# Packing the picks of 32 experts into 27 units of four 32-row strips, in a hybrid attention and mixture-of-experts layer

## What is computed

```python
def hier_moe(h, lw):
    t = h.reshape(B * S, D)
    g_prob, g_idx = lax.top_k(softmax(t @ w_router_group + b_group), 1)
    e_prob, e_idx = lax.top_k(softmax(logit_e_of_that_group), 2)
    weight = g_prob * e_prob / sum(e_prob)
    expert_id = g_idx * 8 + e_idx
    ...
def expert_block(xblk, e):                       # 128 rows, one expert
    hid = silu(xblk @ w_gate[e]) * (xblk @ w_up[e])    # 1024 -> 256
    return hid @ w_down[e]                             # 256 -> 1024
...
y[row_token] += yb * row_weight                  # each token gets two such rows
x = x + gt_m * y
```

## Time and profile before

| | |
|---|---|
| runs | 1118.38 us median of 3 (1114.22 to 3773.64) |
| profiled execution | 1115.39 us, of which the span of the trace is 1113.6 us |
| PE | busy 1042.7 us, 94% of the span |
| DVE, POOL, ACT | busy 57%, 27%, 24% of the span |
| DMA | 229.8 MB, mean 206 GB/s |

### The profile page before, as it was taken

The page is one execution under the profiler, slowest core; times in us unless marked ns, Lnnn a source line. Parts: engine busy times, 40 slices in busy tenths (PEclk is TensorE's granted clock), DMA queues, the critical chain, the costliest instruction groups (busy, mean ns, idle before and its releaser), DMA issues.

```text
span 1113.6 us, 14260 instructions
## 1 busy us (share of the span) xinstructions
PE 1042.7 (94%) x4861; PEld 692.3 (62%) x4861; DVE 632.0 (57%) x1261; ACT 268.0 (24%) x593; POOL 304.1 (27%) x350
## 2 busy tenths in 40 slices
PE   3789999999978899999999999999999999999994
PEld 0334555555556556667776675877777777777772
DVE  1455555555566655675766778456755444445443
ACT  1232222222251232323323212221111111111110
POOL 1122222222231110110110000234445455444444
PEclk9799999999998899999999999799999999999998
DMA  9793333333254322332321129668989999988950
GB/s 306 283 404 125 145 144 145 145 145 126 80 168 130 88 109 97 142 115 67 142 84 59 77 97 389 235 228 345 345 300 351 343 361 345 348 339 341 355 188 18
DMA packets 78102, 229.80 MB, mean 206 GB/s; under 512 B 29835, under 2 KB 33566, under 8 KB 62294
## 3 DMA queue, kind: packets, MB, share of 16 engines
q1 hardware_dynamic: 50608, 198.86, 47.7%
q0 software_dynamic: 24048, 26.81, 7.2%
q10 hardware_dynamic: 3382, 3.32, 0.9%
HBM read 201.23 MB, written 88.25 MB: 260 GB/s over the span
## 4 chain that ended last, share of the span: by engine, by line
PE 81%; DVE 9%; DMA 2%; POOL 2%; issue 2%; ACT 1%; ACTq 1%; DVEq 0%; SPq 0%; POOLq 0%
PE bank L1045 13%; PE bank L1405 10%; PE bank L1407 10%; PE bank L1422 10%; PE bank L998 9%; PE bank L1215 9%; PE bank L1159 6%; PE bank L1185 5%; PE bank L1126 2%; PE bank L1010 2%; PE bank L1026 2%; DMA grope<-in_g_knorm 1%; POOL st L845 1%; PE bank L1056 1%; PE bank L1237 1%
## 5 line engine op out<-in xcount | busy, mean ns | idle before, releaser
L1045 PE MATMUL bank<-W_in,hT 128*128 128x512 f32 (+3 forms) x480 | 172.7, 542 | 3.7 <-DMA W_in<-in_w_in 3.7
L844 POOL TENSOR_SCALAR st<-st 128x1 f32<-128x1 f32 (+5 forms) x76 | 17.6, 231 | 549.6 <-DVEq L1779 251.4
L1045 PEld LDWEIGHTS bank<-W_in,hT 128*128 128x128 f32 (+1 forms) x480 | 80.1, 185 | 91.6 <-issue 84.4
L1422 PE MATMUL bank<-WD,hidT 128*128 128x512 f32 x264 | 118.9, 593 | 1.7 <-DVE hidT L2436 1.7
L1405 PE MATMUL bank<-WG,xT 128*128 128x256 f32 x528 | 119.5, 379 | 1.0 <-DVE xT L2420 1.0
L1407 PE MATMUL bank<-WU,xT 128*128 128x256 f32 x528 | 119.3, 379 | 0.0
L1215 PE MATMUL bank<-W_out,mT 128*128 128x512 f32 (+1 forms) x288 | 115.4, 563 | 0.1
L1407 PEld LDWEIGHTS bank<-WU,xT 128*128 128x128 f32 x528 | 100.3, 190 | 13.6
L1405 PEld LDWEIGHTS bank<-WG,xT 128*128 128x128 f32 x528 | 97.7, 190 | 13.1 <-issue 1.2
L2200 DVE COPY probT<-bank 128x512 f32<-128x512 f32 (+3 forms) x100 | 56.3, 563 | 57.3 <-PE bank L998 50.1
L1185 PEld LDWEIGHTS bank<-vall,probT 128*128 128x128 f32 x616 | 76.8, 192 | 15.6 <-issue 14.6
(11 more groups left out here) (333 smaller groups left out, 1438.0 us busy)
## 6 DMA issues: line engine op xcount, KB each, us to landing
WG<-in_w_gate_e SPq DMA_DIRECT2D x33, 1024.0 KB, 7.0
WU<-in_w_up_e SPq DMA_DIRECT2D x33, 1024.0 KB, 9.4
WD<-in_w_down_e SPq DMA_DIRECT2D x33, 1024.0 KB, 12.9
ada_w<-in_w_ada SPq DMA_DIRECT2D x24, 1024.0 KB, 7.9
residual_scratch<-x_att SPq DMA_DIRECT2D x32, 512.0 KB, 4.4
kbuf<-k_scratch SPq DMA_DIRECT2D x12, 384.0 KB, 5.1
xbuf<-in_x_prompt SPq DMA_DIRECT2D x8, 512.0 KB, 3.8
W_in<-in_w_in SPq DMA_DIRECT2D x2, 2048.0 KB, 22.3
```

Of the source, the lines that this page charges most:

```text
L1045: ins = mm(out, hT[:, place_of[t] % 2, k, :R], W_in[:, k, c0 + c.start:c0 + c.stop], start=(k == 0), stop=(k == KD - 1))
L1422: ins = mm(psum[5 + half][:], hidT[:, k, :], WD[u][:, k, half * 512:(half + 1) * 512], start=(k == 0), stop=(k == 1))
```

## The change

Experts are ranked in each group by their picks in the six early tiles. The expert of rank r in its group gets `CAPS[r]` rows, 160, 128, 128, 128, 96, 96, 64 or 64, that is 27 x 128 rows for all four groups, in place of 32 x 128. The rows of one rank are laid one behind the other over the four groups and cut into units of four strips of 32 rows; the ranks come in the order 1, 6, 0, 2, 4, 7, 3, 5. So 27 units result: 14 of one expert, 7 of two halves (64 rows each), 6 of which one strip belongs to another expert than the other three. Picks beyond an expert's rows go to overflow blocks, up to 24, which all run in the loop; the static 33rd block is gone. What goes with it:

- `gu` and `down` issue one matmul for each run of strips: 128, 64 or 32 columns of the stationary rows, each with its own expert's weights, into the partitions of the bank that belong to these rows. Gate and up weights stand side by side (`WGU`) and are one matmul of 512 columns.
- Units 4, 5, 18 and 19 each bring two new experts, units 15 and 24 too; unit 10 none, the others one. SP reads the expert numbers (`order_i`) in the order `LOADS`, and refills the gate/up half of a slot when the last `gu` of its expert has ended, the down half when the last `down` has.
- DVE picks the early tiles' experts in heads 1 to 3 of the last attention step, PE counts them in head 5 (`rankA`), DVE sorts (`sort_experts`), looks up starts and limits (`expert_rows`) and places the early picks in heads 5 to 7. `place` and `code` get further small instructions.
- There is one copy of the residual rows. POOL gathers a unit's residual rows only when the scatter of each of the three units before it that shares a group with it (under another expert) has landed. The plan never puts such two units side by side; units 5, 6, 18, 19 and 20 have one at distance 2.
- POOL writes 64 more small constants at the start. The MoE part is no longer a loop but written out for all units.

The plan, and the rules for POOL:

```diff
+CAPS = (160, 128, 128, 128, 96, 96, 64, 64)
+RANKS = (1, 6, 0, 2, 4, 7, 3, 5)
+def strip_plan():
+    units, first = [], {}
+    for r in RANKS:
+        strips = [g for g in range(NG) for _ in range(CAPS[r] // STRIP)]
+        first[r] = len(units)
+        units += [[(r, g) for g in strips[i:i + SIDE]] for i in range(0, len(strips), SIDE)]
+    return units, first
+def clashing(m, n):
+    return any(g == h and r != s for r, g in UNITS[m] for s, h in UNITS[n])
...
+        def residual_rows(m):
+            if m >= NG:
+                scattered(m - NG)
+                g.wait_ge(s_ysc[m % NG], 32 * (m // NG))
+            for b in range(max(0, m - NG + 1), m):
+                if clashing(b, m):
+                    scattered(b)
+            rows_in(m % NG, at(TOKEN, m))
+        def gathered_before(m):
+            return max([m - 2] + [b + 1 for b in range(max(0, m - NG + 1), m) if clashing(b, m)])
```

SP and PE:

```diff
-        for z in z_d:
-            sp.dma_start(z[P * t:P * t + R], x_att[:R, s % 2]).then_inc(s_st2[f"x2_{s % 2}"], 16)
+        sp.dma_start(z_d[P * t:P * t + R], x_att[:R, s % 2]).then_inc(s_st2[f"x2_{s % 2}"], 16)
...
+        for q in range(3, len(LOADS)):
+            e = expert(q)
+            if q >= SLOTS:
+                sp.wait_ge(s_gu, LAST_USE[LOADS[q - SLOTS]] + 1)
+            load_gate_up(e, q % SLOTS)
+            if q >= SLOTS:
+                sp.wait_ge(s_down, LAST_USE[LOADS[q - SLOTS]] + 1)
+            load_down(e, q % SLOTS)
...
             for k in range(KD):
-                mm(psum[2][:, 0:DE], xT[:, k, :], WG[u][:, k, :], start=(k == 0), stop=(k == KD - 1))
-            for k in range(KD):
-                ins = mm(psum[3][:, 0:DE], xT[:, k, :], WU[u][:, k, :], start=(k == 0), stop=(k == KD - 1))
+                for c, n, x in runs(UNITS[m]):
+                    ins = mm(out[c:c + n], xT[:, k, c:c + n], WGU[LOADS.index(x) % SLOTS][:, :, k, :], start=(k == 0), stop=(k == KD - 1))
```

DVE, what `place` and `code` get (`place` the first two lines, `code` the rest):

```diff
+            do(TT(over, rankb[:, 0:n], bcast(limit[:].unsqueeze(1), [P, n, NE]), ALU.is_ge))
+            do(STT(rankb[:, 0:n], over, OVER, rankb[:, 0:n], ALU.mult, ALU.add))
...
+            do(V.tensor_copy(ovq_i[:, :, a:b], rank[:, :, a:b]))
+            rows_and_units(ovq_i[:, :, a:b], a, b)
+            do(TT(unit_hot[:, :, a:b], bcast(iota_f[:, 0:NU].unsqueeze(1).unsqueeze(1), [P, 2, n, NU]), bcast(at_f[:, 1, :, a:b].unsqueeze(3), [P, 2, n, NU]), ALU.is_equal))
```

More of the change, by code:

```diff
@@ L113, in free, with runs @@
         return self.freed[self.at[tag][0]]
+def clashing(m, n):
+    return any(g == h and r != s for r, g in UNITS[m] for s, h in UNITS[n])
+assert not any(clashing(m, m) or m and clashing(m, m - 1) for m in range(NU))
+def runs(unit):
+    starts = [i for i in range(SIDE) if i == 0 or unit[i] != unit[i - 1]]
+    width = SIDE if len(starts) == 1 else SIDE // 2 if starts == [0, SIDE // 2] else 1
+    return [(i * STRIP, width * STRIP, unit[i]) for i in range(0, SIDE, width)]
 def overflow_blocks(eng, n_ov, block):
-    with eng.If(n_ov > 1):
-        with eng.Fori(0, MAXOV - 1) as i:
-            with eng.If(i + 1 < n_ov):
-                block(i + 1)
+    with eng.If(n_ov > 0):
+        with eng.Fori(0, MAXOV) as i:
+            with eng.If(i < n_ov):
+                block(i)
             with eng.Else():
@@ L562, in uses @@
             return [("rb", 1)]
+        if work == "rankA":
+            return [("ranks", 1)]
         if work == "x2T":
@@ L835, in _ @@
         do(g.memset(mhalf[:], -0.5))
+        do(g.iota(expert_id[:].rearrange("p (e g) -> p e g", g=NG), [[1, EG], [EG, NG]], base=0, channel_multiplier=0, allow_small_or_imprecise_dtypes=True))
+        for r in range(EG):
+            for group in range(NG):
+                start = P * FIRST_UNIT[r] + CAPS[r] * group
+                do(g.memset(start_of[:, group, r:r + 1], float(start)))
+                do(g.memset(limit_of[:, group, r:r + 1], float(start + CAPS[r])))
         g.sem_inc(s_const, 1)
@@ L1273, in rankA @@
             n = EARLY * NE
-            mm(psum[0][:, 0:n], tri[:], picks(0, EARLY), start=True, stop=True)
-            mm(psum[1][:, 0:n], ones[:], picks(0, EARLY), start=True, stop=True).then_inc(s_ranks, 1)
+            ps = b2.claim(pe, "ranks")
+            mm(ps[:, 0:n], tri[:], picks(0, EARLY), start=True, stop=True)
+            b2.full(mm(ps[:, n:2 * n], ones[:], picks(0, EARLY), start=True, stop=True), "ranks")
         def rankB():
@@ L1434, in overflow_tables @@
                 ins.then_inc(s_sums, 1)
-        def overflow_tokens():
-            pe.wait_ge(s_tab, 4)
-            tr(psum[7][:, 0:P], idf[:, NE:NE + 1].broadcast_to([P, P]), P).then_inc(s_sums, 1)
-        def last_rows():
-            pe.wait_ge(s_yv, 2 * NE)
-            for half in range(2):
-                ins = mm(psum[half][:], same[:], y_end[:, half * 512:(half + 1) * 512], start=True, stop=True)
-            ins.then_inc(s_sums, 1)
         xT4(0, 0, 16)
@@ L1450, in _ @@
         pe.wait_ge(s_gmr, 2)
-        gu(0, 0, 48)
+        gu(0)
         xT4(1, 1, 16)
@@ L2468, in _ @@
         dve.wait_ge(s_sums, 2)
[L2469 removed]
+        decode(slice(0, NU), psum[7][:, NU:2 * NU], psum[7][:, 2 * NU:3 * NU])
         signal(s_tab)
[L2471 removed]
+        for b in range(NU):
             hidT_(b)
[L2473 to L2479 removed]
+            gate(b, b % 2)
+            if b + 1 < NU:
+                hidden(b + 1)
+            if b + 2 < NU:
+                xT_half(b + 2)
+            add_rows(b, b % 2, b % NG, 16 * (b // NG + 1))
             if b == 0:
```

465 lines of the change are left out of this document (226 added, 239 removed).

## The result

The changed kernel takes 1099.88 us (median of four runs, 1097.01 to 1101.16) where the kernel before, run beside it, takes 1116.30 (median of four: 1113.48, 1114.22, 1118.38 and one of 3773.64, which the ratio leaves out): a ratio of 0.986, 95% interval 0.982 to 0.990. That is faster by 1.4%, which is less than the 2% called a difference here, and 25 us above the forecast of 1075. The profiled execution took 1097.01 us with a span of 1095.2, so the sum that was forecast as 1073.4 is to be held against 1095.2.

The account below looks back on a forecast made before the run. PE was taken as the bound, by number of blocks, with DMA nearly full. 1113.6 - 68.6 + 5 + 19 + 2 + 2.4 = 1073.4 us of span, plus 1.8 around it: 1075 us, range 1052 to 1094.

Parts of the forecast that it names:

- Blocks that go: Expert stage: 27 units replace 32 blocks and the static overflow block, 6 x 11.43 = 68.6 us less of PE.
- Form changes, +5: Packed units' matmul groups: 52 changes of tiling form at 0.11 us cost 5 us, bounds 0 and 8.
- fourth rival: Single-strip units: weight loads of strips lie open, 24 of 0.15 us in each of 13 units, 47 us, giving 1112; chance 0.03.
- fifth rival: Packed units: 512-column strips with full operands do not run side by side, 260 us more, giving 1316; chance 0.04.
- Waits for weights, +19: Expert stage: PE waits 10 us for loads at unit 19 and 8 at unit 24, sum 19; ends 13 and 50.
- units 4 and 5 have three full blocks of prefetch behind them, 0 to 2: Expert stage, units 4 and 5: prefetch during three full blocks leaves only 0 to 2 us of weight waits.
- The first rival: Expert stage: loads hide after all, the 19 us of waits falls to 5, giving 1061; chance 0.17.
- The second: Expert stage: DMA bounds the whole stage, needing 342 us from 711 on, giving 1080 to 1092; chance 0.15.
- Residual rows, +2: Units 5, 6, 18, 19, 20: one residual copy makes gathers wait for scatters, 2 us; bounds 0 and 50.
- The last attention step, +1: Heads 1 to 5: 16 us more DVE work fits tightly in 18 us free of 56.5; 1 us, bounds 0 and 6.
- gaps of PE between 600 and 656 us: Last attention step: PE gaps in 600 to 656 us were named as a sign that the prediction is wrong.
- SP and the closing, -2.0 and +3.4: Before the expert stage: DVE work after SP sees heads done comes 2.0 us earlier; longer `code` and `place` cost 3.4.

Follow-up runs that it names:

- k3: Changed kernel loading only the first four experts' weights, later units using what lies in the slots (measurement only): 1069.54 us, stage 328.3 us against 359.0.
- k5: Changed kernel with one full matmul a step in every unit, using its first expert's weights for all strips (measurement only): 1070.53 or 1101.35 us not assigned here; stage 359.1 us.
- k8: Changed kernel with 8, 90 and 30 useless PE matmuls ahead of the weight waits at units 18, 19 and 24: stage 364.8 us against 359.0.
- k14: Changed kernel with 6, 46 and 12 useless PE matmuls ahead of the weight waits at units 18, 19 and 24: 1096.84 us, stage 357.3 us.
- k6: Changed kernel with the same 27 units in an order that spreads those with two experts: 1073.84 us, ratio 0.965 to the kernel before.
- k4: Changed kernel with first-pick rows scattered to an unread copy, so residual gathers wait for no other unit's scatter (measurement only): 1098.73 us, stage 357.6 us.
- k1: Changed kernel with expert order, row starts and limits as constants, sort and lookups left out: 1094.93 us, ratio 0.982 to the kernel before.
- k11: k6 with first-pick rows scattered to an unread copy, so no gather waits for another unit's scatter (measurement only): stage 331.0 us against 332.3.
- k10: Changed kernel with later picks at heads 5 and 6, sort behind the last head, lookups and places in the closing: 1095.13 us, ratio 0.981 to before.
- k12: k10's DVE code with a second spread order of the units, 4 instead of 12 clashing at distance two: 1073.11 us, ratio 0.964 to the kernel before.
- k13: k10's DVE code together with k6's order of units, against the changed kernel: 1075.24 us, ratio 0.965 to the kernel before.

## Why the prediction was wrong

Its own sum, term by term. On the span it missed 21.8 us: 8.2 ahead of the stage, 15.6 in it, and 2.0 the other way behind it.

**Blocks that go: right.** 27 units ran, a full one takes 11.40 us, none overflowed.

**Form changes, +5: right, a little small.** Over the units of k3 the sum above 11.40 is 7 us; k5 shows that it is the form. That is some 0.5 us for a packed unit, about half at each of its two matmul groups, on halves as on strips. The fourth and the fifth rival are refuted: strip matmuls with full operands run four at a time and end when one would. The chain in order of time of the changed kernel shows 7.00 us for the 64 records of strip matmuls of a unit's gate and up, against 6.87 for 16 records of full ones:

```profile
898.71 6.87 PE bank L1477 x16
905.58 0.87 PE bank L1053 x8
906.45 3.44 PE bank L1503 x8
909.89 0.22 PE bank L1053 x2
910.11 7.00 PE bank L1477 x64
```

The rule of the Trainium skill that stood behind the fourth rival (TensorE: Matmul & The Clock Gate, Part 3), that a weight load overlaps a running matmul only if the row group differs, would have made the 7.00 us some 9.3 by an estimate (16 steps with one weight load of 0.15 us in the open each). The measurement decides against it: the strips differ in their columns alone, and full matmuls, which leave no other row group free either, took 6.87 us for 16 records, with no load in the open.

**Waits for weights, +19: wrong in size; the step that failed is "units 4 and 5 have three full blocks of prefetch behind them, 0 to 2" and the silence on what comes behind a wait.** k3 measures the term as 30.7. The two named places were there, 12.2 instead of 10 and 4.4 instead of 8. Beside them stood 6.2 at units 5, 7 and 8 and 1.7 at 18, and 5.6 in the units behind 19 and 24, about 3 of which k8 and k14 show to be the lowered clock. The stage scatters by up to 5 us from trace to trace, so the 11.7 us over the forecast are clear of it. The first rival (loads hidden after all, 1061) did not come. The second (DMA is the bound of the whole stage, 1080 to 1092) fits the number better than the forecast, but its mechanism is refuted: k6 moves the same 32 experts in 332.3 us. What bounds is the order in which experts with few rows are asked for, with four slots.

**Residual rows, +2: small, as forecast.** k4 gives 1.4, within the scatter of the stage; PE never stood behind DVE's sums at the five units named.

**The last attention step, +1: the other step that failed, and beyond its bound.** "It fits, tightly" was counted over 56.5 us with 18 us free. The window was the wrong one. The new work has to go between the copies of head 0 and of head 7, which are 42.1 us apart, and there DVE was free for 42.1 - 30.15 = 12 us, in short waits, the longest of 2.4 us. 12 us of work were added there (42.31 busy). The heads became 10.0 us longer. PE stood for 4.4 of them. The clock, which fell behind each of the two waits (0.93 over 52 us), took some 3.6. The remaining 2 are PE work at full clock, the counting matmuls that moved here among it: k1, whose clock stayed at 1.00, has 43.7 us of PE work in the heads where the kernel before has 42.1. The bound was 6. k1 takes 6.1 us back, 4.4 by the sort and lookups and 1.7 by the clock. The prediction had named gaps of PE between 600 and 656 us as a sign of being wrong, and the first one ended at 632.7.

**SP and the closing, -2.0 and +3.4: about right in size.** SP's first load came 7.1 instead of 7.45 us behind head 7's copy, and from there to the first gate matmul 53.4 instead of 50.0: +3.0 together where 1.4 was forecast. That the 3.4 of the closing are the longer tables is not shown: the clock was low until behind the first gate matmul (0.50 from 705 to 725 us, where the kernel before had 0.82 and then 1.00), and no run separates the two. The whole execution reached the last step 2.4 us earlier than that of before, which is scatter of the start.

**First unit and end: not in the sum.** The first unit's gate and up took 9.95 us instead of 7.14, since the clock was still at its lower level (0.65 in 722 to 732). Of the 3.9 us by which k3's stage exceeds my 324.4, this is 2.8. Behind the last down 2.0 us less than before remained. So 8.2 + 11.7 + 3.9 - 2.0 = 21.8.

**The chances.** 0.89 for faster by 2% took the whole 0.58 of the forecast as faster, and so rested on the ends of two terms not being reached together. Both passed their middle, by 9 and 12 us. Some 3.6 us of the one and 3 of the other have a reason in common, to which the sum gave no term: a PE that waits, even for 2 us, can also lose its clock.

## What to carry to other kernels

Where a faster engine has to be fed through a few slots, look at the demand per unit and not at the total. Two units that need two loads each stood side by side here, PE waited 12 us for the second, and another order of the same units gave some 23 us back, more than the change itself had brought (16). To ask whether an engine has room for added work, take the stretch between the two events that bound it, head by head, not the window that is at hand. And do not count a wait or work removed beside a nearly full queue as won: k5 and k11 took 7 and 6 us away, 4 and 3 of them came back as waits for weights, and the stages, on one trace each, are within the scatter of what they were.

## What was not expected of the hardware

TensorE's granted clock fell to half (1.2 instead of 2.4 GHz) behind waits as short as 0.9 to 2.2 us in a stretch where PE was otherwise busy, and not every time: three profiled executions with the same instructions and the same 0.9 us wait (k10, k12, k13) had 0.66, 1.00 and 0.74 over the 20 us around and behind it, and 5 to 7 us hung on it. A wait of 1.9 us for head 3's probabilities was followed by a lowered clock in the changed kernel and by none in k1. Matmuls without use ahead of a wait kept it at 1.00 over 100 us (k8, k14) where it had been 0.95.

Four matmuls of 512 columns on strips of 32 stationary columns run side by side at full operand size: 7.00 us for 64 records of them, 6.87 for 16 of full ones.
